# One core, hybrid diffusion backbone of two layers: the experts' last scatter accumulates in PSUM, layer 1's first norm is applied by diagonal products, and products without a reader run on TensorE

## The reference, cut to what matters

```python
h = rmsnorm(x, g_pre1[l]) * (1.0 + sc1) + sh1
y, y_c = token_mixers(h, hc, w_in[l], ..., ctx_out)
x = x + gt1 * rmsnorm(y, g_post1[l])
h2 = rmsnorm(x, g_pre2[l]) * (1.0 + sc2) + sh2
x = x + gt2 * rmsnorm(expert_choice_ffn(h2, w_router[l], w_e1[l], w_e3[l], w_e2[l]), g_post2[l])
```

## Time and profile before

| | |
|---|---|
| median of 3 runs | 1936.45 us (1934.49 to 1937.45) |
| profiled execution | 1932.31 us, its span 1930.5 us |
| instructions in the span | 21557 |
| TensorE busy | 1680.1 us, 87% |
| VectorE, ScalarE, GpSimd busy | 584.1, 327.0, 98.4 us |
| moved by DMA | 525.15 MB, mean 272 GB/s |
| chain that ended last | TensorE 61%, DMA 33%, VectorE 4%, ScalarE 1% |

### The profile page before, as it was taken

The page is one execution under the profiler, slowest core; times in us unless marked ns, Lnnn a source line. Parts: engine busy times, 40 slices in busy tenths (PEclk is TensorE's granted clock), DMA queues, the critical chain, the costliest instruction groups (busy, mean ns, idle before and its releaser), DMA issues.

```text
span 1930.5 us, 21557 instructions
## 1 busy us (share of the span) xinstructions
PE 1680.1 (87%) x9087; PEld 876.0 (45%) x9087; DVE 584.1 (30%) x1078; ACT 327.0 (17%) x776; POOL 98.4 (5%) x174
## 2 busy tenths in 40 slices
PE   6999999999997998979888799999996767776765
PEld 2656445444476432424222266777884323232222
DVE  3744334464664111112111523444113111010102
ACT  3213334200023010101001321343012000000001
POOL 5001100000021000000000000110000000000000
PEclk9999999999998999999999999999998887686677
DMA  9632005143485899999999941205757999999996
GB/s 356 208 123 39 1 1 197 60 180 134 150 324 216 338 401 421 421 421 421 421 421 421 398 135 59 38 9 186 242 219 298 421 420 421 421 421 421 421 421 256
DMA packets 130667, 525.15 MB, mean 272 GB/s; under 512 B 9886, under 2 KB 73532, under 8 KB 75276
## 3 DMA queue, kind: packets, MB, share of 16 engines
q1 hardware_dynamic: 127884, 520.47, 68.2%
q0 software_dynamic: 2688, 3.32, 1.0%
HBM read 522.70 MB, written 1.05 MB: 271 GB/s over the span
## 4 chain that ended last, share of the span: by engine, by line
PE 61%; DMA 33%; DVE 4%; ACT 1%; issue 1%; SPq 0%; DVEq 0%; ACTq 0%
DMA ring<-in_w_e_dram 32%; PE ps L826 14%; PE ps L1125 10%; PE ps L1305 8%; PE ps L1164 4%; PE ps L1134 4%; PE ps L1085 3%; PE ps L1327 3%; PE ps L729 2%; PE ps L1047 2%; PE ps L1257 2%; PE ps L945 2%; PE ps L1285 1%; DMA ring<-in_w_mod_dram 1%; PE ps L1069 1%; PE ps L922 1%
## 5 line engine op out<-in xcount | busy, mean ns | idle before, releaser
L1305 PE MATMUL ps<-ring,arena 128*32 128x256 f32 (+1 forms) x2856 | 382.9, 515 | 100.5 <-DMA ring<-in_w_e_dram 97.1
L1327 PE MATMUL ps<-ring,arena 128*32 128x256 f32 (+1 forms) x1496 | 219.5, 567 | 71.5 <-DMA ring<-in_w_e_dram 69.1
L1305 PEld LDWEIGHTS ps<-ring,arena 128*32 128x32 f32 (+1 forms) x2856 | 124.4, 130 | 337.0 <-DMA ring<-in_w_e_dram 162.7
L1125 PE MATMUL ps<-arena,ring 128*128 128x512 f32 (+1 forms) x576 | 191.7, 486 | 0.0
L826 PE MATMUL ps<-arena,ring 128*128 128x512 f32 (+1 forms) x480 | 177.2, 525 | 0.0
L1327 PEld LDWEIGHTS ps<-ring,arena 128*32 128x32 f32 (+1 forms) x1496 | 69.6, 140 | 216.5 <-issue 108.8
L2120 DVE COPY arena<-ps 32x512 f32<-32x512 f32 (+1 forms) x128 | 70.9, 554 | 278.6 <-PE ps L1327 277.3
L1125 PEld LDWEIGHTS ps<-arena,ring 128*128 128x128 f32 x576 | 109.2, 190 | 75.7 <-issue 68.3
L1668 ACT ACTIVATE arena<-ps 128x512 f32<-128x512 f32 (+1 forms) x32 | 15.7, 491 | 729.1 <-PE ps L1305 729.1
L2113 DVE TENSOR_TENSOR arena<-arena,ps 128x512 f32<-128x512 f32 (+1 forms) x32 | 17.8, 555 | 372.9 <-PE ps L1305 372.9
L826 PEld LDWEIGHTS ps<-arena,ring 128*128 128x128 f32 x480 | 89.9, 190 | 84.1 <-issue 80.3
(11 more groups left out here) (221 smaller groups left out, 1375.7 us busy)
## 6 DMA issues: line engine op xcount, KB each, us to landing
ring<-in_w_e_dram SPq DMA_DIRECT2D x364, 1024.0 KB, 17.8
ring<-in_w_in_dram SPq DMA_DIRECT2D x44, 1024.0 KB, 9.2
ring<-in_w_mod_dram SPq DMA_DIRECT2D x40, 1024.0 KB, 12.7
arena<-in_w_e_dram SPq DMA_DIRECT2D x17, 1024.0 KB, 7.9
ring<-in_w_out_dram SPq DMA_DIRECT2D x8, 1024.0 KB, 10.8
arena<-in_w_mod_dram SPq DMA_DIRECT2D x8, 1024.0 KB, 14.7
arena<-in_w_br_ml_dram SPq DMA_DIRECT2D x8, 512.0 KB, 5.9
arena<-in_w_br_mla_dram SPq DMA_DIRECT2D x8, 256.0 KB, 2.7
```

Source lines behind the costliest of these rows:

```text
L1125: mm = pe.matmul(ps[:, u % 3, tq], wg[:, k, cols], hT[:, k, tq], start=k == 0, stop=k == KD - 1)
L1305: mm = pe.matmul(ps[M * j:M * j + M, m, 0:NW], XSTs[l][e // GROUP % 2][:, kk, e % GROUP, 0:M], w[:, k, j * NW:(j + 1) * NW], start=kk == 0 ...
L1327: mm = pe.matmul(ps[M * j:M * j + M, 3, 0:NW], lhs, w[:, k, j * NW:(j + 1) * NW], start=kk == 0, stop=kk == KD - 1)
```

## The change

The last group's scatter no longer goes through SBUF. Products with the identity put Ya's sums into the eight banks (four in layer 1) during the last two experts, as banks come free, and the scatter products add onto them. Half of the last expert's copies to Yg moves from VectorE to ScalarE. ScalarE squares from PSUM; VectorE multiplies PSUM by the gate row, then by the root, and adds X in the same pass. At the start of layer 1 the rows are not scaled and turned: a product of X with a diagonal matrix of the reciprocal roots does both. ScalarE's norm statistics of layer 1 stand between the last statistics of layer 0. Modulation group 5 moves from the start of layer 1 to layer 1's merge, on VectorE and for the latent stream only. Products into bank 1 that nothing reads are put behind the router's turns of both layers and into the last expert of layer 1.

```diff
-SUMMED = {2: 6, 3: 15}
+SUMMED = [{2: 6, 3: 15}, {5: 6}]
...
-    loads = [("mod", *MOD_GROUPS[5 if layer else 0], k) for k in range(KD)]
+    loads = [("mod", *MOD_GROUPS[0], k) for k in range(KD)] if layer == 0 else []
...
-    return order[:-4] + pick(SPARE_ORDER[2][:3]) + order[-4:] + pick(SPARE_ORDER[2][3:]) + ring[:4] + pick(SPARE_ORDER[3]) + \
+    return order[:-4] + pick(SPARE_ORDER[2][:2]) + order[-4:] + pick(SPARE_ORDER[2][2:]) + ring[:4] + pick(SPARE_ORDER[3]) + \
...
                 elif name == "ctx_rows":
-                    sp.wait_ge(sem("n1_xn"), before("n1_xn", l) + 4)
+                    sp.wait_ge(sem("h1_tr"), 2 * 2)
...
-                pool.wait_ge(sem("n1_tr"), before("n1_tr", l) + KD)
+                if l:
+                    pool.wait_ge(sem("x_post2"), 4)
+                else:
+                    pool.wait_ge(sem("n1_tr"), KD)
...
+            def keep_busy(n, cols):
+                for _ in range(n):
+                    pe.matmul(ps[:, 1, 0:cols], ident[:, :], X[:, 3, 0:cols], start=True, stop=True)
...
-                    for k in range(KD):
-                        mod_product(5, k)
-                if l:
-                    norm_turn(l, 1, xn1, range(4))
-                    mod_turn(5)
+                    for t in range(4):
+                        pe.wait_ge(sem("diag_ready"), t + 1)
+                        for k in range(KD):
+                            mm = pe.matmul(ps[:, post_bank(t) + k // 4, k % 4 * P:(k % 4 + 1) * P], X[:, t, k * P:(k + 1) * P],
+                                           diag[:, t, :], start=True, stop=True)
+                            if k % 4 == 3:
+                                mm.then_inc(sem("h1_tr"), 1)
+                    pe.wait_ge(sem("h1_act"), 3)
+                    pe.wait_ge(sem("h1_dve"), 5)
...
                 mm.then_inc(sem("affT_tr"), 1)
+                keep_busy(6, 512)
...
                 mm.then_inc(sem("rank_tr"), 1)
+                keep_busy(3, 256)
...
+                def sums_into_banks(os):
+                    for o in os:
+                        si, c2, half = o // 4, (o // 2) % 2, o % 2
+                        mm = pe.matmul(ps[:, final_bank(L, o), :], ident[:, :],
+                                       Ya[:, 2 * L.streams[si] + c2, half * 512:(half + 1) * 512],
+                                       start=True, stop=False, skip_group_check=True)
+
+                def last_scatter():
+                    pe.wait_ge(sem("y_taken"), before("y_taken", l) + N_EXP)
+                    pe.wait_ge(sem("y_half"), l + 1)
+                    for o in range(NB_):
+                        si, c2, half = o // 4, (o // 2) % 2, o % 2
+                        if o == 7:
+                            sums_into_banks((7,))
+                        pe.matmul(ps[:, final_bank(L, o), :], GT[:, si, c2 * P:(c2 + 1) * P], Yg[:, si, half * 512:(half + 1) * 512],
+                                  start=False, stop=True, skip_group_check=True).then_inc(sem("scattered"), 1)
...
                 def expert_out(e):
+                    if e == N_EXP - 1 and L.ns == 2:
+                        sums_into_banks((4, 5))
                     pe.wait_ge(sem("hidT_ready"), before("hidT_ready", l) + e + 1)
+                    if e == N_EXP - 1 and L.ns == 2:
+                        sums_into_banks((6,))
...
                         mm.then_inc(used, 1)
+                        if e == N_EXP - 1 and l == 1:
+                            keep_busy(1, 512)
...
                         expert_in(e, 1)
+                    if e == N_EXP - 1:
+                        pe.wait_ge(sem("gt_ready"), before("gt_ready", l) + GROUPS)
+                        pe.wait_ge(sem("g2_taken"), before("g2_taken", l) + 2 * L.ns)
+                        pe.wait_ge(sem("ya_added"), before("ya_added", l) + 1 + NB_ * (GROUPS - 1))
+                        sums_into_banks(range(4))
...
-                scatter(GROUPS - 1)
-                if l == 0:
-                    pe.wait_ge(sem("ya_added"), 8 * GROUPS + 1)
+                last_scatter()
```

ScalarE's part (`stat_next` is the wait for an X tile and `norm_stat`; `h1_bank` is four activations of 128x128 from PSUM to hT, with scale and shift columns):

```diff
+                    for t in range(1, 4):
+                        h1_bank(t, 1)
...
+                    if u == 17:
+                        mod_cols(5 if l else 2)
...
+                    if e == N_EXP:
+                        act.wait_ge(used, expert_load(l, N_EXP - 1, 2, 3) + 1)
+                        for j in range(2, 4):
+                            si, at = y_piece(L, j)
+                            ins = copy(Yg[3 * CAP:4 * CAP, si, at:at + NW], ps[j * CAP:(j + 1) * CAP, 3, 0:NW])
+                        ins.then_inc(sem("y_half"), 1)
...
+                def post_last(j):
+                    act.wait_ge(sem("scattered"), before("scattered", l) + 4 * L.ns * (GROUPS - 1) + 2 * (j + 1))
+                    b = final_bank(L, 2 * j)
+                    at = stat[:, 40 + L.chunks[j]:41 + L.chunks[j]]
+                    act.activation(junk2, ps[:, b:b + 2, :].rearrange("p b n -> p (b n)"), ACT.Square, accum_out=at)\
+                        .then_inc(sem("post2_squared"), 1)
+                    act.wait_ge(sem("post2_squared"), before("post2_squared", l) + j + 1)
+                    rstd(at, at, D).then_inc(sem("post2_rstd"), 1)
...
+                if l == 0:
+                    post_last(0)
+                    post_last(1)
+                    stat_next(0)
+                    post_last(2)
+                    stat_next(1)
+                    post_last(3)
+                    stat_next(2)
+                    stat_next(3)
+                else:
+                    post_last(0)
+                    post_last(1)
```

VectorE's part (`diagonal(t)` waits for the reciprocal root of tile t and multiplies the identity by it; `h1_bank` is four passes of 128x128 from PSUM; `mod_streams(5)` is the latent stream alone):

```diff
+                    if u == 15:
+                        mod_row(5 if l else 2)
                     for o, k in mods_summed(l, u):
                         mod_part(o, k)
...
-                        for j in range(4):
+                        for j in range(4 if e < N_EXP else 2):
...
-                scatter_add(GROUPS - 1)
-                dve.wait_ge(sem("ya_added"), before("ya_added", l) + NB_ * GROUPS + 1)
-                for j, t in enumerate(L.chunks):
-                    post(2, j, t, Ya, G2s[l], tmp2s[l])
+                def scaled(j):
...
+                    dve.wait_ge(sem("post2_squared"), before("post2_squared", l) + j + 1)
+                    b = final_bank(L, 2 * j)
+                    own(dve.tensor_tensor(Ya[:, t, :], ps[:, b:b + 2, :].rearrange("p b n -> p (b n)"), G2s[l][:, t // 2, :], ALU.mult))
+
+                def residual(j):
...
+                    dve.wait_ge(sem("post2_rstd"), before("post2_rstd", l) + j + 1)
+                    dve.scalar_tensor_tensor(out=X[:, t, :], in0=Ya[:, t, :], scalar=stat[:, 40 + t:41 + t], in1=X[:, t, :],
+                                             op0=ALU.mult, op1=ALU.add).then_inc(sem("x_post2"), 1)
+
+                for j in range(2):
+                    scaled(j)
+                    residual(j)
                 if l == 0:
+                    diagonal(0)
+                    scaled(2)
+                    residual(2)
+                    diagonal(1)
+                    scaled(3)
+                    residual(3)
+                    diagonal(2)
+                    h1_bank(0, 0)
+                    h1_bank(0, 1)
+                    h1_bank(1, 0)
+                    diagonal(3)
+                    h1_bank(2, 0)
+                    h1_bank(3, 0)
```

More of the change, by code:

```diff
@@ L101 @@
     hid_ready=N_EXP, hid_tr=N_EXP, hidT_ready=N_EXP, y_taken=N_EXP,
-    scattered=32, ya_added=33,
+    scattered=32, ya_added=25, post2_squared=4,
 )
@@ L366, in backbone @@
         G2s = [view(8192, 2, D), view(7168, 2, D)]
-        tmp2s = [view(10240, D), view(9216, D)]
         junk2 = view(18432, D)
+        diag = view(19456, 4, P)
         aff = view(22016, 4, N_EXP)
@@ L751, in mod_sum, with merge_mods @@
                 pe.wait_ge(sem("mod_row"), o)
-                for s in range(2):
+                streams = mod_streams(o)
+                for s in streams:
                     for j in range(4):
                         mm = pe.matmul(ps[32 * j:32 * j + 32, 6, :], pick[:, s, :], acc[s][:, 512 * j:512 * j + 512],
-                                       start=s == 0, stop=s == 1, skip_group_check=True)
+                                       start=s == streams[0], stop=s == 1, skip_group_check=True)
                 mm.then_inc(sem("mod_summed"), 1)
-            def merge_mods(u):
-                if u == 7:
+            def merge_mods(l, u):
+                if l == 0 and u == 7:
                     mod_turn(1)
-                for o, first in SUMMED.items():
+                for o, first in SUMMED[l].items():
                     if u == first + KD:
@@ L875, in parts_of @@
                     for k in range(KD):
-                        if ready:
+                        if ready and l == 0:
                             pe.wait_ge(sem("n1_lat"), before("n1_lat", l) + k + 1)
@@ L1436, in _ @@
                     act.wait_ge(sem("x_loaded"), 32)
```

(13 more changed lines are left out.)

105 lines of the change are left out of this document (47 added, 58 removed).

## The result

The changed kernel takes **1920.26 us** (median of 4 runs, 1919.29 to 1922.65) against 1935.77 for the kernel before (4 runs, 1934.49 to 1937.45): a ratio of 0.9931 on record, 95% interval 0.9918 to 0.9944, so faster by 0.7%. The quotient of the two medians is 0.9920, which lies in the same interval. The forecast, 1924.6 of 1936.45, is a ratio of 0.9939, inside the interval too; the measured time is inside the stated range of 1919 to 1931, near its lower end.

A forecast was written before the change was run, and what follows sets the result against it. Experts were taken as DMA-bound, layer 1's merge as TensorE-bound, with savings ahead of the DMA's hole counting. Terms -1.0 - 0.7 + 0.0 - 7.9 + 1.6 - 3.8 = -11.8 us, giving 1924.6 from 1936.45; range 1919 to 1931.

The forecast's parts named there:

- Routers: Routers of both layers: idle products fill TensorE's waits and speed the gathers; -1.0 us in layer 0, -0.7 in layer 1.
- a hole in the transfers: Between merge and experts, 1467 to 1475 us, DMA moves 8 GB/s; TensorE savings ahead of it move the whole expert stage.
- Turn: Turn from layer 0 to layer 1, last expert product to first gate products: 24.3 us against 32.2, -7.9.
- the first of the eight additions on the path: Turn of the layer: VectorE's eight additions go, of which only the first was taken to be on the path.
- inside the bounds: Turn: ScalarE's square of 1024 columns from PSUM bounded by 1.0 and 1.5 us, taken as 1.16.
- the rival in which it falls: TensorE's clock falls at the turn: 4.3 us less gain, -7.5 in all, 1928.9 us; chance 0.22.
- Merge: Layer 1's merge: a sum over partitions and four turns come on TensorE's path, +1.6 us.
- the rival that ends slower, VectorE as the merge's bound: Layer 1's merge: eight VectorE sums, 18.8 us, go on the path; +7.0 in all, 1943.4 us; chance 0.05.
- the one of half its size: Layer 1's merge: four odd units each wait one sum, 9.4 us; -2.4 in all, 1934.1 us; chance 0.06.
- End: Layer 1's end, last product to last row of X: 9.3 us against 13.1, -3.8; -2.2 at the low clock.
- Layer 1's experts: Four sums are recouped in seven waits for landings, then added products keep TensorE at work between the last quarters; no cost.

The follow-up runs named there:

- e8: Changed kernel with the fourth diagonal made earlier, fillers (products without a reader) at the turn, and none behind the last expert's quarters: 1917.37 us, 0.9915 of the kernel before.
- e5: Changed kernel with the fourth diagonal made after VectorE's first bank of hT, plus fillers at the turn of the layer: 1918.37 us, 0.9921 of the kernel before.
- e6: Kernel before with only the nine products without a reader in each router added: 1928.50 us, 0.9972 of the kernel before.
- e3: Changed kernel with 14 fillers instead of 6 behind the first turn of each router: 1931.99 us, 0.9986 of the kernel before.
- e1: Changed kernel without the routers' fillers, those in the last expert kept: 1922.44 us, 0.9938 of the kernel before.
- e9: Changed kernel with layer 0's last scatter added to the sums by VectorE again: 1925.39 us, 0.9956 of the kernel before.
- e7: Kernel before with only layer 1's end added in PSUM, squared and scaled from there; copies left to VectorE, no fillers: 1932.24 us, 0.9990 of the kernel before.
- e10: Changed kernel with all four copies behind the last expert on VectorE again, in both layers: 1923.58 us, 0.9948 of the kernel before.
- e2: Changed kernel without the fillers behind the last expert's quarters in layer 1: 1921.92 us, 0.9933 of the kernel before.
- e11: e8 with small products without a reader added in the waits of layer 1's router ahead of the affinities: 1917.39 us, 0.9916 of the kernel before.

## Why the prediction was right, step by step

**Routers: right in kind, layer 1 undersized.** Layer 0 gave 1.66 for 1.0, because the old gather's 9.34 us were compared with four groups of 2.08, and its 64 instructions take 7.80 in a row. Layer 1 gave 2.25 for 0.7: of the six fillers about 1.3 were slow and not 2.4 (6.57 us instead of 7.6), so the rank's turn was hardly late. That term, missed by 1.55 us, varies: the six took 8.02 and 8.08 us in e8 and e5. That it counts, since it lies ahead of a hole in the transfers, is shown by e6 and e3.

**Turn: right in size, and the steps hold; the closeness is luck.** 24.33 for 24.3, with the last diagonal after 20 us and groups of 2.05. The forecast was for the full clock, at which the same turn takes 23.67 (e1; 23.68 in e3). ScalarE's squares and statistics follow each other by 1.6 us and not 1.72, so the last diagonal was made at 20.0 and not 20.7; the low clock then put back 0.7. ScalarE is in the chain where the forecast had it, and VectorE is close to it. Of the 7.8 us, 4.9 are the additions (e9) and 1.4 the halved copies; the other 1.5 (the diagonals in place of turn and norm, less 0.7 by the clock) were not separated. One reading of before was wrong: the forecast has the first of the eight additions on the path. Before's own timeline of VectorE has all eight there, the first scaled row right behind the last of them:

```profile
1094.83 0.69 DVE L2099 TENSOR_TENSOR arena<-arena,ps 128x512 f32<-128x512 f32 x1 [0.17 <-PE ps L1285]
1095.55 1.28 DVE L1993 SCALAR_TENSOR_TENSOR arena<-arena,stat 128x1024 f32<-128x1024 f32 x1
```

It did no harm, as the forecast added up the new turn from its own steps and took the old one's length as measured. The square of 1024 columns straight from PSUM, which no row showed, took 1.02 and 0.19 for its sum, inside the bounds. In the clock, the rival in which it falls came true in part, from the last diagonal group on, at 2.4 us of the 4.3 priced. The same products behind the same waits held the clock in e1 and e3. Whether the execution decides that, or the edits of e1 and e3 in the router of layer 0, 480 us earlier, is not shown: the four profiles in which it fell all have the router's fillers as changed. The page "TensorE: Matmul & The Clock Gate" of the Trainium skill says, in the section "Part 1: The HAM clock gate (the "warmup" mystery)", that the number of slow products at a kernel's start varies from run to run; the traces here show the like in the middle of one (7.13 us in before and 8.68 in e7 for the same scatter at the turn, which e7 leaves as it was).

**Merge: right.** 1.97 for 1.6. TensorE's two added pieces, in its timeline:

```profile
1371.10 1.06 PE L763 MATMUL ps<-arena,pick 128*32 128x512 f32 x8
...
1381.70 0.63 PE L732 MATMUL ps<-ident,rows 128*128 128x128 f32 x4
```

They make 1.69; the rest is one short wait and starts. TensorE waits for no modulation sum, so the rival that ends slower, VectorE as the merge's bound, did not come, nor the one of half its size.

**End: right in size, in part for another reason.** -3.99 for -3.8. With the scatter at 3.70 us in both, e6's end of 11.56 against 9.20, the change gives 2.4, of which 1.5 are PSUM (e6 against e10) and 0.9 the halved copies (e10 against after). The other 1.6 are that the scatter of before happened to run slowly in the profile, and the forecast took that profile's slow scatter as the kernel's. Its own terms add up to 9.2 us, not the 9.3 that it gives.

**Layer 1's experts: +1.94 instead of 0.** The step that failed is that the fillers there keep TensorE at work "between the last quarters", at no price: when the clock is low at their start, the quarter ahead takes 1.94 us for 1.07 and the first filler 2.05 for 1.13, and the quarters fall behind the landings. In e3, where all of them ran at the full clock, the stage took 437.57 us, as before. The sum had 0.0 for it.

**The sum.** It is 2.2 us off between the traces (-9.6 for -11.8), by misses of both signs: +1.9 in layer 1's experts and +1.8 from the gate products to the merge (the low clock) against -2.2 in the routers. Between the medians the change is -13 by the ratio and -15.5 by the difference, more than forecast. Between one profile and another the same code differed by 1.3 us at before's turn (32.15; 33.45 in e6, 33.43 in e7), by 1.6 at its end and by 2.4 at the changed turn. Before's profile had the short turn and after's the low clock behind it, 3.7 of the gap; before's slow end works the other way by 1.6. So the gap between traces and medians is of the size of these differences, and is not closed by them; that the forecast's 1924.6 lies 4.3 above the measured median stays open to that extent.

## What to carry to other kernels

A saving ahead of a hole in the transfers moves everything behind it, as the routers' fillers alone showed (0.9972), while a filler among products that wait for landings must be shorter than the wait even at the low clock. At a serial turn between stages, follow the chain from engine to engine and take whole passes off it: an accumulation in PSUM in place of eight additions ahead of the first row (4.9 us) and copies halved between two engines (1.4) counted in full. Before a gain of a microsecond or two is put into a sum, ask at which clock the row ran from which it is read; another execution of the same code may have the other.

## What the runs showed of the hardware

TensorE's clock at the same place of the same code differs between executions. The scatter at before's turn took 7.13 us in before and 8.68 in e7, behind the same wait of 2.89; e7's edits come into play only later, at layer 1's end. Between kernels that differ in some other place it was 2.05 or 2.71 us for a group of sixteen diagonal instructions behind the same wait of 1.97 (e1, after), and 3.70 or 5.40 for the eight of the added scatter behind waits of 0.98 and 0.97 (e2, e11). Small products without a reader in the waits of layer 1's router went with six fast long ones behind them in the one profile that has them (e11: 5.32 us, elsewhere 6.44 to 8.08). Squaring 1024 columns from PSUM takes ScalarE 1.02 us, a little less than the 1.06 from SBUF (both in the kernel after).
